# The last team of a mixture-of-experts stage: its sum split over pairs and row groups, and its last weights loaded in another order

## The reference, cut to what matters

```python
x = x + merged @ p["w_out"]
x = x + hierarchical_moe(rmsnorm(x, p["g_ffn"]), p)

def hierarchical_moe(h, p):            # gate: (tokens, 32), two entries per token are not zero
    ...
    y = jnp.zeros_like(h)
    for e in range(N_EXPERTS):
        hid = jax.nn.silu(h @ p["w_e1"][e]) * (h @ p["w_e3"][e])
        y = y + gate[..., e:e + 1] * (hid @ p["w_e2"][e])
    return y
```

## Time and profile before

| | us |
|---|---|
| median of 3 runs (lowest, highest) | 646.52 (645.71, 647.54) |
| the profiled execution, its own time | 645.93 |
| its span, from the first to the last instruction | 644.1 |
| TensorE busy in the span | 611.7 |
| TensorE's granted clock, mean | 0.999 of full |
| mean transfer rate over the span, GB/s | 233 |

### The profile page before, as it was taken

The page is one execution under the profiler, slowest core; times in us unless marked ns, Lnnn a source line. Parts: engine busy times, 40 slices in busy tenths (PEclk is TensorE's granted clock), DMA queues, the critical chain, the costliest instruction groups (busy, mean ns, idle before and its releaser), DMA issues.

```text
span 644.1 us, 9883 instructions
## 1 busy us (share of the span) xinstructions
PE 611.7 (95%) x3674; PEld 378.5 (59%) x3674; DVE 329.3 (51%) x878; ACT 170.9 (27%) x540; POOL 149.7 (23%) x341
## 2 busy tenths in 40 slices
PE   9999999999999999999999999998999999986785
PEld 6788867776556667666677767853443343332341
DVE  2434846868874588783133322675435335334233
ACT  5534234321678433221100101121221121120100
POOL 1695726733584433410000000000000000000000
PEclk9999999999999999999999999999999999999999
DMA  9783553222301523323389991098999999999993
GB/s 301 176 284 115 193 159 99 66 67 93 101 2 33 168 95 99 99 66 98 107 236 404 399 386 64 10 383 345 417 417 413 418 416 417 417 418 417 416 409 126
DMA packets 61681, 150.55 MB, mean 234 GB/s; under 512 B 12352, under 2 KB 40448, under 8 KB 53696
## 3 DMA queue, kind: packets, MB, share of 16 engines
q1 hardware_dynamic: 61632, 149.89, 62.7%
HBM read 147.12 MB, written 2.76 MB: 233 GB/s over the span
## 4 chain that ended last, share of the span: by engine, by line
PE 83%; SPq 9%; DVE 4%; DMA 2%; ACT 1%; issue 1%
PE PS L819 30%; PE PS L829 20%; SPq L704 6%; PE PS L1188 5%; PE PS L1096 5%; PE PS L1227 3%; SPq L708 3%; PE PS L1217 3%; DMA E<-in_w_e 2%; PE PS L943 2%; PE PS L966 2%; PE PS L894 2%; PE PS L883 1%; PE PS L800 1%; PE PS L1008 1%; PE PS L951 1%
## 5 line engine op out<-in xcount | busy, mean ns | idle before, releaser
L819 PE MATMUL PS<-hT,W 128*128 128x320 f32 x448 | 125.9, 436 | 0.0
L819 PEld LDWEIGHTS PS<-hT,W 128*128 128x128 f32 x448 | 83.6, 190 | 37.5 <-issue 5.2
L1188 PE MATMUL PS<-E,xT 128*32 128x256 f32 x1024 | 58.6, 379 | 9.5 <-issue 8.4
L1188 PEld LDWEIGHTS PS<-E,xT 128*32 128x32 f32 x1024 | 35.4, 110 | 36.9 <-issue 20.4
L2152 POOL TENSOR_SCALAR means<-sums 128x4 f32<-128x4 f32 (+3 forms) x35 | 7.9, 225 | 189.2 <-ACT junk L1325 188.2
L1096 PE MATMUL PS<-h,S 128*128 128x512 f32 (+1 forms) x96 | 48.2, 625 | 0.7 <-DVE S L1939 0.7
L1227 PE MATMUL PS<-yb,WG 128*128 128x512 f32 (+1 forms) x96 | 40.9, 622 | 4.0 <-DVE X L2080 3.1
L829 PE MATMUL PS<-W,hT 128*128 128x256 f32 (+5 forms) x256 | 41.7, 353 | 0.0
L2080 DVE TENSOR_TENSOR X<-X,PS 128x512 f32<-128x512 f32 (+1 forms) x48 | 32.9, 686 | 8.3 <-PE PS L1227 6.7
L829 PEld LDWEIGHTS PS<-W,hT 128*128 128x128 f32 (+1 forms) x256 | 31.5, 163 | 8.4 <-issue 1.3
L829 PE MATMUL PS<-W,mergedT 128*128 128x384 f32 (+3 forms) x192 | 35.7, 381 | 0.0
(11 more groups left out here) (313 smaller groups left out, 959.0 us busy)
## 6 DMA issues: line engine op xcount, KB each, us to landing
E<-in_w_e SPq DMA_DIRECT2D x93, 1024.0 KB, 21.8
W<-in_w_in SPq DMA_DIRECT2D x7, 1536.0 KB, 7.2
W<-in_w_in SPq DMA_DIRECT2D x7, 1024.0 KB, 6.6
W<-in_w_mem_kv SPq DMA_DIRECT2D x4, 1024.0 KB, 6.1
W<-in_w_glu SPq DMA_DIRECT2D x4, 768.0 KB, 8.0
W<-in_w_out SPq DMA_DIRECT2D x2, 1536.0 KB, 15.4
E<-in_w_e SPq DMA_DIRECT2D x6, 512.0 KB, 18.8
X<-in_x_prompt SPq DMA_DIRECT2D x4, 512.0 KB, 4.4
```

Source lines behind the costliest of these rows:

```text
L819: ins = mm(out[:, 0:TOK], w[:, k, cols:cols + 128], rhs[:, k, :], start=(k == 0), stop=(k == kt - 1))
L1188: ins = mm(PS[r:r + B, 2 + par, 0:FF], xT[:, k, place_ + B * n:place_ + B * n + B], E13[slot][:, :, k, 128 * j:128 * j + 128], start=(k == ...
```

## The change

Five things are changed, all for the last pair or team.

- **Order of loads.** The up weights of expert 30 are issued behind the down weights of experts 28 and 29 instead of ahead of them. Those of expert 31 are split 6 to 2 over the eight k blocks, instead of 4 to 4.
- **Early part of the sum.** Before `up(15)`, TensorE puts the rows so far into PSUM (an identity times the left half of `X`) and adds the first pair of the team (pair 14, 64 places) for tiles 2 and 0. Tile 1 follows in two pieces, around `hid_transpose(15)`.
- **The last pair's `down`** writes the four quarters of its result to two banks, so that each bank has the left or right quarter of both halves on all 128 partitions. `y_copy` then copies 128x256 instead of 64x512, into `last_rows`.
- **The last products** take 64 places each: the left half of the columns on the array's rows 0 to 63 (with `last_weights`, a second copy of the weights, moved down by 64 partitions), the right half on rows 64 to 127.
- **The end.** ScalarE copies the left halves to `X`, VectorE adds the right halves, and each of the six pieces is stored for itself.

```diff
-    return (6, 7, 0, 1, 2)[m - LAST_SUMS] if m >= LAST_SUMS else 6 + m % len(SUMS) % 2
+    return 6 + m % len(SUMS) % 2
+LAST_TILES = (2, 0, 1)
+LAST_BANKS = {(2, 0): (6, 0), (2, 1): (6, 64), (0, 0): (7, 0), (0, 1): (0, 0), (1, 0): (1, 0), (1, 1): (2, 0)}
+LAST_K = 6
...
-                for k0, k1 in ((0, KD),) if e < NE - 1 else ((0, KD // 2), (KD // 2, KD)):
+                for k0, k1 in ((0, KD),) if e < NE - 1 else ((0, LAST_K), (LAST_K, KD)):
...
+                for e in ups:
+                    if e != NE - 2:
+                        load_up(e)
...
+                for e in downs:
+                    load_down(e)
+                if NE - 2 in ups:
+                    load_up(NE - 2)
...
+                    for half, bank_ in enumerate((5, 4)):
+                        for c in range(2):
+                            for n, slot in enumerate(slots):
+                                r, at = 64 * c + B * n, 512 * c + 256 * half
+                                ins = mm(PS[r:r + B, bank_, 0:256], hidT[:, par, 64 * n + B * j:64 * n + B * j + B],
+                                         E2[slot][:, j, at:at + 256], start=(j == 0), stop=(j == 1))
...
+            def rows_so_far():
+
+                pe.wait_ge(s["sum_added"], ADDS * (TEAMS - 1))
+                pe.wait_ge(s["weights_ready"], TEAMS)
+                pe.wait_ge(s["weights_moved"], 1)
+                for t in LAST_TILES:
+                    n = TILES[t][1]
+                    mm(last_place(t, 0), ident[0:n, 0:n], X[0:n, t, 0:512], start=True, stop=False)
+
+            def add_last_but_one(t, c):
+                f, n = TILES[t]
+                mm(last_place(t, c), WG[0:64, f:f + n], yb[0:64, c, :], start=(c == 1), stop=False)
+
+            def add_last():
+                pe.wait_ge(s["last_y"], 2)
+                for t in LAST_TILES:
+                    f, n = TILES[t]
+                    for c, weights in enumerate((last_weights[:, f:f + n], WG[64:128, f:f + n])):
+                        mm(last_place(t, c), weights, last_rows[64 * c:64 * c + 64, :], start=False, stop=True).then_inc(s["last_full"], 1)
...
+                    rows_so_far()
+                    pe.wait_ge(s["y_dve"], PAIRS - 1)
+                    pe.wait_ge(s["y_act"], PAIRS - 1)
+                    for t in LAST_TILES[0:2]:
+                        for c in range(2):
+                            add_last_but_one(t, c)
                 up(p)
+                if p == PAIRS - 1:
+                    add_last_but_one(LAST_TILES[2], 0)
...
+                if p == PAIRS - 1:
+                    add_last_but_one(LAST_TILES[2], 1)
                 down(p)
-            add_team(TEAMS - 1, range(len(SUMS)))
+            add_last()
...
+                if g == TEAMS - 1:
+                    fn(last_weights, PS[64:128, 7, 0:TOK], ACT.Copy).then_inc(s["weights_moved"], 1)
...
+                if p == PAIRS - 1:
+                    fn(last_rows[:, 256:512], PS[:, 4, 0:256], ACT.Copy).then_inc(s["last_y"], 1)
...
+                fn(X[0:n, t, 0:512], PS[r:r + n, bank_, :], ACT.Copy).then_inc(s["last_act"], 1)
...
-            add_team(TEAMS - 1, range(len(SUMS)))
+                V_.tensor_tensor(X[0:n, t, 512:D], X[0:n, t, 512:D], PS[r:r + n, bank_, :], ALU.add).then_inc(s["last_dve"], 1)
```

More of the change, by code:

```diff
@@ L765, in _ @@
                 sp.wait_ge(s["ov_done"], OV_TEAMS + 1)
-            for n, (t, cs) in enumerate(SUMS):
+            for i, t in enumerate(LAST_TILES):
                 f, rows_ = TILES[t]
-                sp.wait_ge(s["sum_added"], added_by(len(SUMS) * (TEAMS - 1) + n))
                 dst = o["y_p"][f:f + rows_, :] if t < 2 else o["y_s"]
-                c0, c1 = 512 * cs[0], 512 * cs[-1] + 512
-                store(dst[:, c0:c1], X[0:rows_, t, c0:c1])
+                for c, by in enumerate(("last_act", "last_dve")):
+                    sp.wait_ge(s[by], i + 1)
+                    store(dst[:, 512 * c:512 * c + 512], X[0:rows_, t, 512 * c:512 * c + 512])
             st.after(stored[-1])
@@ L1205, in down, with last_down, down_products @@
                     pe.wait_ge(s["y_act"], p)
-                second = (s["last_down_loaded"], 16) if p == PAIRS - 1 else None
-                down_products([(2 * p + n) % DOWNS for n in range(2)], p % 2, second).then_inc(s["y_mm"], 1)
-            def down_products(slots, par, second=None):
+                slots = [(2 * p + n) % DOWNS for n in range(2)]
+                (last_down if p == PAIRS - 1 else down_products)(slots, p % 2).then_inc(s["y_mm"], 1)
+            def last_down(slots, par):
                 for j in range(2):
-                    if j == 1 and second is not None:
-                        pe.wait_ge(*second)
+                    if j == 1:
+                        pe.wait_ge(s["last_down_loaded"], 16)
+                    for half, bank_ in enumerate((5, 4)):
[4 more added lines that the diff above has]
+                                         E2[slot][:, j, at:at + 256], start=(j == 0), stop=(j == 1))
+                return ins
+            def down_products(slots, par):
+                for j in range(2):
                     for c in range(2):
@@ L1563, in _ @@
             act.wait_ge(s["ov_ready"], 2)
+            for i, t in enumerate(LAST_TILES):
+                bank_, r = LAST_BANKS[t, 0]
+                n = TILES[t][1]
+                act.wait_ge(s["last_full"], 2 * i + 2)
+                fn(X[0:n, t, 0:512], PS[r:r + n, bank_, :], ACT.Copy).then_inc(s["last_act"], 1)
             teams = act.value_load(ovi[0:1, OV_TEAMS * TEAM:], min_val=0, max_val=OV_TEAMS)
@@ L2100, in _ @@
             teams = dve.value_load(ovi[0:1, OV_TEAMS * TEAM:], min_val=0, max_val=OV_TEAMS)
-            add_team(TEAMS - 1, range(len(SUMS)))
+            for i, t in enumerate(LAST_TILES):
+                bank_, r = LAST_BANKS[t, 1]
+                n = TILES[t][1]
+                dve.wait_ge(s["last_full"], 2 * i + 2)
+                V_.tensor_tensor(X[0:n, t, 512:D], X[0:n, t, 512:D], PS[r:r + n, bank_, :], ALU.add).then_inc(s["last_dve"], 1)
             with dve.If(teams > 0):
-                dve.wait_ge(s["sum_added"], ADDS * TEAMS)
+                dve.wait_ge(s["last_act"], NT)
+                dve.wait_ge(s["last_dve"], NT)
                 with dve.Fori(0, OV_TEAMS) as i:
```

33 lines of the change are left out of this document (19 added, 14 removed).

## The result

The changed kernel takes 650.16 us, median of 6 runs (649.39 to 650.72), where the kernel before took 646.12, median of 6 (645.57 to 647.54). The ratio is 1.0056, with a 95% interval of 1.0046 to 1.0067. A second set of runs gave 649.83 beside 646.92, ratio 1.0045 (1.0032 to 1.0058). So the change costs 3 to 4 us. The difference between the sets lies mostly in the kernel before: the median of six, 646.12, falls between three runs at 645.57 to 645.71 and three at 646.52 to 647.54, and the larger sets of 23, 23 and 35 runs have medians of 646.97, 646.92 and 646.73. The profiled execution after took 649.86 of its own time.

What follows compares the result with a forecast made beforehand. Weights bound the expert stage, then a 12 us tail; after the change TensorE sets `up(15)`'s start. +4.2 late copies - 0.3 copy - 1.7 slots + 0.5 stores = +2.7 us; forecast 649.0 us, range 647.0 to 651.6.

Steps and rivals of the forecast that it cites:

- Loads: Weight stream: new order keeps it full and ending as before; `down(14)` starts at 621.60, a gain of 0.43 us.
- Ahead of `up(15)`: TensorE from 621.60: `down(14)`, rows so far and first pair (2.96 us each) start `up(15)` at 629.43, 4.0 us late.
- Behind it: After `up(15)`: tile 1's left half fits the pause, its right half delays `down(15)` to 635.51; copies 4.2 us late.
- slots: TensorE's unit of price: one of the two MATMUL rows of a 512 column product, 0.43 us.
- changes: TensorE: extra cost where the products' shape changes, taken as 0.19 us each, 0.15 for the low end.
- Given back: After `down(15)`: shorter copy gives 0.3 us, last products of 6 slots instead of 10 give 1.7, taking 3.0 us.
- The stores: SP's queue at the end: six issues instead of five, the last 0.5 us behind its data, costing +0.5 us.
- The two halves of tile 2 do not collide: Rival, last products: tile 2's halves in one bank take turns, two slots more, 0.9 us, 649.9; chance 0.15.
- The row groups run at once, six slots and not twelve: Forecast, last products: 6 slots. Rival without overlap: 12 slots, +2.6 us, 651.6; chance 0.12.
- The changes of shape are not hidden: Rival, TensorE: changes of shape mostly hidden and stores don't jam, +1.3 us, 647.8; chance 0.15.
- A product over 64 rows takes a whole slot: Rival, TensorE: such a product takes half a slot, 3.4 us less, change wins 0.7 us, 645.8; chance 0.04.

Runs made afterwards that it cites:

- Experiment 4: Changed kernel with its three identity products (the rows so far) run twice in a row; 652.48 us, ratio 1.0092 to the kernel before.
- experiment 6: Changed kernel without the loop for rows that don't fit and the four jumps over it; 649.72 us, ratio 1.0039 to the kernel before.
- experiment 5: Changed kernel with one store for the tile of 64 rows instead of two, five issues instead of six; 650.41 us, ratio 1.0062 to the kernel before.
- experiment 3: Changed kernel without the identity products for the rows so far, VectorE adding all six pieces; 646.88 us, ratio 1.0004 to the kernel before.
- experiment 7: Changed kernel without identity products, pair 14 laid out in two row groups like pair 15, VectorE making six adds; 646.74 us, ratio 0.9991.
- experiment 8: Experiment 7's version plus one identity product for tile 0's left half, copied by ScalarE, VectorE making five adds; 646.77 us, ratio 1.0007 to the kernel before.
- experiment 9: Loop for rows that don't fit and its jumps left out: of the kernel before, 645.97 us (ratio 0.9997); of experiment 8's version, 645.91 us (0.9994).
- experiment 2: Kernel before with only the new load order and 6 to 2 split, plus two unread identity products filling the pause; 646.68 us, ratio 1.0004.

## Why the prediction was right, and which term was off

It said 649.0 us, from a sum of +2.7 us and a span of 646.8. Measured were 650.16 us, +4.0 in the first set and +2.9 in the second, and a span of 648.0. Of the 1.2 us between the two spans, 0.74 are the lateness of the whole trace, which no term of the sum could foresee, 0.68 are the stores, and 0.26 go the other way. Point by point, with the times after less the 0.74 by which that whole trace is late:

- **Loads.** `down(14)` at 621.60, as worked out. That the new order costs nothing holds in this kernel, but on a ground that I had not named: something must fill the pause. Alone, with the pause open, it cost 1.1 us.
- **Ahead of `up(15)`.** From start to start it is 2.92 us for the rows so far and 2.91 for the first pair, 2.96 worked out for each. `up(15)` starts at 629.28, 629.43 worked out. Experiment 4 shows that this stretch is on the path in full.
- **Behind it.** The left half of tile 1 in the pause cost next to nothing (from its start to the transpose it is 1.11 us, where the pause was 1.03; the prediction's own prices, two slots and two changes from 633.06, come to 634.30, past the 634.12 into which it should just fit); from the transpose to `down(15)` it is 1.31 us, 1.39 worked out. The copies start at 637.29, 637.50 worked out, 4.0 us later than before.
- **Given back.** The copy and the start behind it take 0.48 us instead of 0.57, the last products 3.04 instead of 3.0. In all the tail grew by 1.98 us, 2.24 predicted.
- **The stores.** This is the term that was mis-sized: +0.5 us predicted, +1.18 measured. SP's last issue starts 0.9 us behind its data and not 0.5, and 0.3 come behind it. The queue is behind in both traces of the changed kernel and in experiment 6 (0.9 each). The 0.3 are the difference of two traces that both have a read of code among their stores, so they are not its whole price: without it the kernel before is 0.8 to 1.0 us quicker there. Either way the changed form loses 0.9 to 1.3 us there (5.49 and 5.73 beside 4.55 with the read, 4.85 beside 3.51 and 3.79 without). In experiment 5 saving an issue didn't help. With the pieces free one by one the stores take 3.18 us without the read (experiment 3) and 4.67 with it (experiment 7), less than the changed form in either case. That the spacing by itself does it was not tried apart from the rest.
- **Rivals.** The two halves of tile 2 do not collide: they start at 638.51 and 638.52 and take 0.64 us each, their second rows start at 638.99 and 639.00, and the next tile follows 1.01 us after the first row, two slots and a change. Tile 0's two halves in two banks start together in the same way, at 639.52. The Trainium skill, TensorEngine Tiling (Array Packing), "Gotcha 1: PSUM Pressure", states that different row tiles can't access the same bank at once. Here they do so on different partitions, and the measurement decides. The row groups run at once, six slots and not twelve. The changes of shape are not hidden: 12 slots of 0.43 are 5.16, and with four changes the two groups take 5.83. A product over 64 rows takes a whole slot.

What the mechanism comes to: the last weights set the time at which the tail may begin, and the kernel before had about 2.2 us of waits ahead of them. The change moved 5.9 us of products there, to take 1.7 away at the end. Experiments 7 and 8 put 2.1 and 3.1 us there in place of it (counted from the first early product to `up(15)`), and end level with the kernel before. None of the ten other versions is faster than it by more than can be told.

What stays open is why the stores take longer in the changed form with and without the read, and what the loop's jumps are worth in each kernel. In the one version where it was measured in the same set (experiments 8 and 9) leaving them out gave 0.86 us; in the changed kernel it gave 0.1 in medians of 5 runs, and in the kernel before 0.8, which its interval doesn't set apart from nothing.

## What to carry to other kernels

Before moving work ahead of a wait, add up the pauses there and price the work in the same rows: here 2.2 us of pause were offered 5.9 us of products, and a doubling of the moved part shows at once whether it is on the path. What such a move saves at the end (here 1.7 us) must be more than what overflows the pause (here 4.0). And at the end of a kernel count the transfers apart from the last result: how far apart the pieces come free, and what else reads through the same transfer engines, was 1.18 of the 3.16 us that the change lost between the traces, and leaving out a jump gave one version 0.86.

## What the runs showed of the hardware

- **Two row groups of the array run at once in float32,** also into one PSUM bank on different partitions: twelve rows of 64x512 in 3.04 us, where twelve slots one behind the other took 5.83 (624.19 to 630.02). A change of shape costs 0.17 us in the mean of the four between 624.19 and 630.02, and one of columns alone 0.15, in the last products (638.51 to 639.52, less two slots).
- **The clock falls behind some pauses.** Behind 3.04 or 3.05 us of pause the 64 rows of `up(13)` took 3.66 us in one trace and 5.00 to 6.54 in eleven, behind 2.31 us `up(15)` took 5.35. Behind 1.71 and 1.77 us `down(12)` took 3.57 and 3.59 us in two traces (experiment 2, and the kernel before without the loop), behind 1.76 in another 1.92; behind the pauses of 0.62 and 0.68 in the earlier trace rows its halves took the 1.93 us of full speed. Of all traces only the first had a mean clock of 0.999; the others had 0.991 to 0.996.
- **The jumps over code that isn't run go with a read of code.** Left out together, they took the read among the stores away in all three kernels (experiments 6 and 9); which of the four makes it was not tried. TensorE's jump over the loop took 3.3 to 3.7 us where the read fell among the stores and 0.5 to 0.9 where it did not, and the read went through a transfer engine that carries the stores. In four of the eight traces with such a read one issue of a store took 1.2 to 1.9 us instead of 0.3 to 0.7, and the slowest store landed 4.1 us after its issue instead of 3.4 in the kernel before, 4.2 and 4.4 instead of 3.5 in the changed one.
